# Factor rows written by transposes, and scores and weighings of stick-breaking attention taken in groups

## The reference, cut to what matters

```python
def rmsnorm_2(x, gain):
    y = xf * lax.rsqrt(jnp.mean(xf * xf, axis=-1, keepdims=True) + EPS)
    return (y * gain.astype(jnp.float32)).astype(x.dtype)

def stick_breaking_attention(q, k, v):      # (B, H, S, dh)
    for t0 in range(0, seq, Q_BLOCK):       # Q_BLOCK = 128
        t1 = t0 + Q_BLOCK
        z = jnp.einsum('bhqd,bhkd->bhqk', q[:, :, t0:t1], k[:, :, :t1]) * scale
        causal = jnp.arange(t1)[None, :] < (t0 + jnp.arange(Q_BLOCK))[:, None]
        log_stay = jnp.where(causal, jax.nn.log_sigmoid(-z), 0.0)
        log_between = lax.cumsum(log_stay, axis=3, reverse=True) - log_stay
        weights = jnp.where(causal, jnp.exp(jax.nn.log_sigmoid(z) + log_between), 0.0)
        outs.append(jnp.einsum('bhqk,bhkd->bhqd', weights, v[:, :, :t1]))

def stick_breaking_mixer(h, w_qkv, q_gain, k_gain, w_o):
    q, k, v = jnp.split(h @ w_qkv, 3, axis=-1)
    q = rmsnorm_2(q.reshape(bsz, seq, SB_HEADS, SB_HEAD_DIM), q_gain)
    k = rmsnorm_2(k.reshape(bsz, seq, SB_HEADS, SB_HEAD_DIM), k_gain)
    ...
    return o @ w_o
```

## Time and profile before

| | |
|---|---|
| median of three runs | 1926.21 us |
| the profiled execution's own time | 1931.22 us |
| its span, first to last instruction | 1929.4 us |
| TensorE busy in the span | 1885.6 us (98%) |
| VectorE busy | 1062.4 us (55%) |
| ScalarE busy | 840.9 us (44%) |
| GpSimd busy | 1084.4 us (56%) |
| mean granted TensorE clock | 0.996 of full speed |

### The profile page before, as it was taken

The page is one execution under the profiler, slowest core; times in us unless marked ns, Lnnn a source line. Parts: engine busy times, 40 slices in busy tenths (PEclk is TensorE's granted clock), DMA queues, the critical chain, the costliest instruction groups (busy, mean ns, idle before and its releaser), DMA issues.

```text
span 1929.4 us, 28543 instructions
## 1 busy us (share of the span) xinstructions
PE 1885.6 (98%) x10584; PEld 1586.1 (82%) x10584; DVE 1062.4 (55%) x1911; ACT 840.9 (44%) x1514; POOL 1084.4 (56%) x1321
## 2 busy tenths in 40 slices
PE   7998999999999999999999999999999999999998
PEld 6887777888888877777888889878887888899887
DVE  6548675632123366676756565385745576555552
ACT  4554444532233356565543444343333354444441
POOL 5327333445557433334788888654333268888882
PEclk9999999999999999999999999999999999999999
DMA  6214212223333311112233333333222133232331
GB/s 184 62 33 121 55 46 58 63 71 98 99 104 109 88 56 55 55 45 70 84 103 106 100 99 100 102 95 88 60 61 66 45 98 99 88 110 88 97 112 55
DMA packets 269163, 160.43 MB, mean 83 GB/s; under 512 B 6137, under 2 KB 267489, under 8 KB 268898
## 3 DMA queue, kind: packets, MB, share of 16 engines
q1 hardware_dynamic: 269026, 158.61, 28.5%
HBM read 156.50 MB, written 2.10 MB: 82 GB/s over the span
## 4 chain that ended last, share of the span: by engine, by line
PE 87%; POOL 5%; DVE 4%; ACT 3%; issue 2%; DMA 0%; SPq 0%; ACTq 0%; DVEq 0%
PE bank L259 20%; PE bank L1999 9%; PE bank L623 7%; PE bank L625 7%; PE bank L624 7%; POOL weight_lo L241 3%; PE bank L1600 3%; PE bank L2644 3%; PE bank L2646 3%; PE bank L2645 3%; PE bank L425 2%; PE bank L1602 2%; PE bank L1601 2%; PE bank L427 2%; PE bank L426 2%
## 5 line engine op out<-in xcount | busy, mean ns | idle before, releaser
L241 POOL TENSOR_TENSOR weight_lo<-weight_stage,weight_hi 128x256 fp32r<-128x256 f32 x1160 | 960.9, 862 | 764.0 <-ACT weight_hi L229 764.0
L229 ACT ACTIVATE weight_hi<-weight_stage 128x1024 fp32r<-128x1024 f32 (+2 forms) x303 | 309.1, 1022 | 254.7 <-PE bank L259 181.8
L259 PE MATMUL bank<-hidden_hi,weight_lo 128*128 128x512 f32 x512 | 200.4, 391 | 4.9 <-POOL weight_lo L241 4.9
L623 PE MATMUL bank<-a_hi,weight_lo 128*128 128x512 f32 (+1 forms) x464 | 198.8, 428 | 1.6 <-DVE a_lo_rounded L1137 1.0
L259 PE MATMUL bank<-hidden_lo,weight_hi 128*128 128x512 f32 x512 | 199.4, 389 | 0.0
L259 PE MATMUL bank<-hidden_hi,weight_hi 128*128 128x512 f32 x512 | 199.2, 389 | 0.0
L625 PE MATMUL bank<-a_hi,weight_hi 128*128 128x512 f32 (+1 forms) x464 | 182.8, 394 | 0.0
L624 PE MATMUL bank<-a_lo_rounded,weight_hi 128*128 128x512 f32 (+1 forms) x464 | 182.6, 394 | 0.0
L1975 POOL TENSOR_TENSOR block_weight_lo<-block_weight,block_weight_hi 128x256 fp32r<-128x256 f32 x156 | 124.7, 832 | 52.6 <-ACT block_weight_hi L2134 52.6
L2349 DVE TENSOR_TENSOR x_t<-x_t,bank 128x512 f32<-128x512 f32 x128 | 82.1, 678 | 90.4 <-PE bank L259 90.4
L259 PEld LDWEIGHTS bank<-hidden_hi,weight_lo 128*128 128x128 f32 x512 | 96.1, 188 | 26.1 <-issue 6.9
(11 more groups left out here) (393 smaller groups left out, 4407.3 us busy)
## 6 DMA issues: line engine op xcount, KB each, us to landing
weight_stage<-in_mlp_w SPq DMA_DIRECT2D x128, 512.0 KB, 3.8
weight_stage<-in_w_in SPq DMA_DIRECT2D x57, 512.0 KB, 3.7
weight_stage<-in_hg_w_in SPq DMA_DIRECT2D x32, 512.0 KB, 3.9
weight_stage<-in_sb_w_qkv SPq DMA_DIRECT2D x24, 512.0 KB, 3.6
weight_stage<-in_w_mkv SPq DMA_DIRECT2D x8, 512.0 KB, 3.8
weight_stage<-in_w_out SPq DMA_DIRECT2D x8, 512.0 KB, 3.9
weight_stage<-in_sb_w_o SPq DMA_DIRECT2D x8, 512.0 KB, 3.7
weight_stage<-in_hg_w_o SPq DMA_DIRECT2D x8, 512.0 KB, 3.7
```

Source lines behind the costliest of these rows:

```text
L229: act.activation(self.hi[slot][:, 0:size], self.stage[slot][:, 0:size], ACT.Copy).then_inc(self.hi_done, 1)
L241: last = pool.tensor_tensor(self.lo[slot][:, part], self.stage[slot][:, part], self.hi[slot][:, part].bitcast(F32), ALU.subtract)
L259: last = pe.matmul(out, l, r, start=n == 0, stop=n == 3 * len(pairs) - 1)
L623: pe.matmul(to, wlo, ahi(k), start=k == 0, stop=False)
```

## The change

In all four places that write factor rows `pe.matmul(to, column, eye, ...)` becomes `pe.transpose(to, column, eye)`; operands and results are the same. In stick-breaking, `score` of block 0 also does the scores of block 1 of the same pair, which go beside it in the bank (from column 128), and there is no score in step i = 0. TensorE's `weigh` runs in steps with i = 1 and i = 3 alone, for steps m-3 and m-2, right behind the score. VectorE masks four items in step i = 3 and none in step i = 0; `lower` moves from step i = 1 to i = 3, `put` on ScalarE from i = 0 to i = 2. Waits count accordingly.

```diff
@@ FoldedNorm.pe_spread
         for i in range(NT):
-            last = pe.matmul(self.bank[:, i * P:(i + 1) * P], self.rstd[:, i:i + 1].to_broadcast([P, P]), self.S.eye,
-                             start=True, stop=True)
+            last = pe.transpose(self.bank[:, i * P:(i + 1) * P], self.rstd[:, i:i + 1].to_broadcast([P, P]), self.S.eye)
@@ Columns.spread, spread_k and spread_out: the same edit
...
@@ stick_breaking, TensorE
+        def score_at(i):
+            return P if i == 1 else 0
...
                 wait(pe, sig, 4 * m)
-                for a in range(0, (i + 1) * P, 2 * P):
...
+                for i in (0, 1) if i == 0 else (i,):
+                    for a in range(0, (i + 1) * P, 2 * P):
...
+                            last = pe.matmul(score_banks[r][:, score_at(i) + a:score_at(i) + b],
+                                             qt[p % 3][rows, i * P:(i + 1) * P],
+                                             kt[p % 3][rows, a:b], start=True, stop=True)
...
-                if m + 1 < M:
+                if m + 1 < M and i:
                     score(m + 1)
+                if i % 2 and m >= 3:
+                    weigh(m - 3)
+                    weigh(m - 2)
                 fill(3 if some == 3 else 3 - some)
...
-                if m >= 1:
-                    weigh(m - 1)
...
+            weigh(M - 2)
             weigh(M - 1)
@@ VectorE
-                dve.wait_ge(scored, n + 1)
+                dve.wait_ge(scored, n + 3 if i == 0 else n + 1)
...
-                if i == 1 and p >= 1:
+                if i == 3 and p >= 1:
                     lower(p - 1)
                 weigh(2 * m)
-                if m + 1 < M:
-                    mask(2 * m + 2)
-                    mask(2 * m + 3)
+                if m + 1 < M and i:
+                    for n in range(2 * m + 2, 2 * m + (6 if i == 3 else 4)):
+                        mask(n)
                 weigh(2 * m + 1)
@@ ScalarE
-                act.wait_ge(masked, n + 1)
+                act.wait_ge(masked, n + 3 if i == 0 else n + 1)
...
-                if i == 0 and p >= 1:
+                if i == 2 and p >= 1:
                     put(p - 1)
```

More of the change, by code:

```diff
@@ L481, in spread @@
         for i in range(count):
-            last = pe.matmul(bank[0:rows, i * P:(i + 1) * P], self.rstd[:, first + i:first + i + 1].to_broadcast([P, rows]),
-                             self.S.eye, start=True, stop=True)
+            last = pe.transpose(bank[0:rows, i * P:(i + 1) * P],
+                                self.rstd[:, first + i:first + i + 1].to_broadcast([P, rows]), self.S.eye)
         return last
@@ L1629, in spread_k @@
                 for i in range(NT):
-                    last = pe.matmul(aux[:, i * P:(i + 1) * P], wide[:, i * P:(i + 1) * P], S.eye, start=True,
-                                     stop=True)
+                    last = pe.transpose(aux[:, i * P:(i + 1) * P], wide[:, i * P:(i + 1) * P], S.eye)
                 last.then_inc(spread, 1)
@@ L1645, in score @@
                 wait(pe, sig, 4 * m)
-                for a in range(0, (i + 1) * P, 2 * P):
[L1647 to L1653, removed]
+                for i in (0, 1) if i == 0 else (i,):
+                    for a in range(0, (i + 1) * P, 2 * P):
+                        b = min(a + 2 * P, (i + 1) * P)
+                        for r in range(2):
+                            rows = slice(r * 64, r * 64 + 64)
+                            last = pe.matmul(score_banks[r][:, score_at(i) + a:score_at(i) + b],
+                                             qt[p % 3][rows, i * P:(i + 1) * P],
+                                             kt[p % 3][rows, a:b], start=True, stop=True)
+                            if b == (i + 1) * P:
+                                last.then_inc(scored, 1)
             def turn(n):
@@ L1782, in vector @@
             scale_k(0)
-            mask(0)
-            mask(1)
+            for n in range(4):
+                mask(n)
             for m in range(M):
@@ L1856, in sigmoids @@
                 p, a = h // 2, T - (i + 1) * P
-                src = score_banks[n % 2][:, 0:(i + 1) * P]
-                act.wait_ge(masked, n + 1)
+                src = score_banks[n % 2][:, score_at(i):score_at(i) + (i + 1) * P]
+                act.wait_ge(masked, n + 3 if i == 0 else n + 1)
                 wait(act, turned, n - 3)
@@ L2715, in spread_out @@
                 for c in range(NT):
-                    last = pe.matmul(aux[:, c * P:(c + 1) * P], rstd[:, h % 2 * NT + c:h % 2 * NT + c + 1].to_broadcast([P, P]), S.eye,
-                                     start=True, stop=True)
+                    last = pe.transpose(aux[:, c * P:(c + 1) * P],
+                                        rstd[:, h % 2 * NT + c:h % 2 * NT + c + 1].to_broadcast([P, P]), S.eye)
                 last.then_inc(spread, 1)
```

2 lines of the change are left out of this document (1 added, 1 removed).

## The result

| | before | after |
|---|---|---|
| median, six runs each | 1929.17 us | 1913.39 us |
| lowest and highest | 1925.66 and 1932.79 | 1906.42 and 1917.26 |
| ratio, with its 95% interval | | 0.9914 [0.9888, 0.994] |
| the profiled execution | 1931.22 us | 1908.62 us |
| idle TensorE in stick-breaking | 2.04 us | 4.75 us |

The changed kernel is faster by 0.9%, where 1.3% was forecast: 1913.4 us against 1902.0, and 2.4 us beyond the upper end of the range. The two profiled executions are 22.6 us apart, near the 24.2 of the sum. Two executions, one of e1_rows_only (7012 us at a granted clock of 0.255) and one of the kernel before beside it (9250 us at 0.191), are left out of all figures.

What follows compares the result with a forecast made beforehand. TensorE, busy in 98% of the span, was taken to bound the kernel. 13.4 + 11.8 - 1.0 = 24.2 us off 1931.2 gives 1907.0, less 5.0 for the runs' median: 1902.0 us, range 1897 to 1911.

Steps and rivals of the forecast that it cites:

- the 24.2 of the sum: Whole kernel: factor rows 13.4 us plus groups 11.8 us, less 1.0 us for waits, gives 24.2 us saved.
- Four calls: Factor rows: a spread of four calls costs 0.88 us as matmuls and should cost 0.44 us as transposes.
- a score of blocks 0 and 1: Stick-breaking: the grouped score costs about 1.04 us with one fixed part, saving 0.40 us in each of 8 pairs.
- one direct neighbour: Stick-breaking: a product right behind a score saves one form change, 0.19 us in 14 places, 2.7 us; bounds nothing to 5.3.
- that rival: Stick-breaking: VectorE's moved work stalls every pair at `turn` in step i = 0, losing 12 us, ending at 1913 us; chance 0.08.
- the prediction's own signs of being wrong: TensorE waiting for VectorE in early pairs, a group with more than one fixed part, or a stage clock under 1.00.
- what it was plus 0.9 us: Outside stick-breaking: TensorE's idle time stays as before, but for 0.9 us more at 146 to 163 us.
- the sum was 15.3 us before waits: Stick-breaking: the forecast's terms there, 3.5 us from spreads and 11.8 us from groups.
- 1.0 charged: Stick-breaking: TensorE's waits go from 2.0 to 3.0 us; bounds a gain of 2.0 us and a loss of 4 us.
- What is late next is VectorE: Stick-breaking: VectorE's weights for `turn` come up to 1.5 us later, covered up to pair 5, not fully in pairs 6 and 7.
- a chance as a disaster: Rival: each of 33 transpose groups sets off a clock fall of 1.7 us, costing 55 us, ending at 1957 us; chance 0.02.
- The median of the runs is 5.0 us lower: Base: 5.0 us taken off the profiled execution's forecast of 1907.0 us, to predict a median of 1902.0 us.

Runs made afterwards that it cites:

- e1_rows_only: Kernel before with only the factor rows written by transposes instead of float32 matmuls; 1919.5 us, ratio 0.9939.
- e7: Changed kernel with one projection step put between the score and the products with v behind it; 1914.19 us, ratio 0.9917 to the kernel before.
- e5: Changed kernel with GpSimd waiting, ahead of splitting weight unit 25, until VectorE has made its first two biases; 1907.29 us.
- e9: Kernel before with only GpSimd's wait for VectorE's first two biases added; 1925.31 us, ratio 0.9966.
- e12: Changed kernel with scores one step at a time as before, products with v still grouped, factor rows by transposes; 1912.32 us.
- e8: Changed kernel with scores still grouped, but products with v one step at a time as before; 1914.03 us.
- e4: Changed kernel measured once more, without edits, beside other variants; 1908.45 us, ratio 0.9891 to the kernel before.
- e2: Changed kernel with the factor rows written by float32 matmuls again, so the groups alone; 1925.44 us, ratio 0.996 to the kernel before.
- e3: Changed kernel with groups up to pair 5 and the old order in pairs 6 and 7; 1913.43 us, ratio 0.9897 to the kernel before.
- e6: Changed kernel with, in the last pair, transposes of v ahead of the score and `put` and `lower` a step earlier; 1908.89 us.

## Why the prediction was right and where it was wrong

**Right: the mechanism, and nearly every price.** TensorE's list of work set the end. Four calls cost 0.44 us; a score of blocks 0 and 1 costs 1.05 us with one fixed part (1.71 with its six transposes in e7, less 0.66; forecast about 1.04); products for blocks 2 and 3 alone 1.87 (1.84); one direct neighbour saves 0.18 to 0.20 (0.19). No early pair waits for VectorE, so that rival is out. One of the prediction's own signs of being wrong did come: the clock of the stage is 0.99. Idle time outside the stage did not stay what it was plus 0.9 us either: it fell from 41.8 to 38.4 us, and 3.2 us of that is TensorE's wait for the held addition, which of the two profiles only before's has. So the question is what the 24.2 us left out.

**Terms that were left out or too small.** In the stage the sum was 15.3 us before waits; 10.39 came.

- Waits: 1.0 charged. Idle time went from 2.04 to 4.75 us, which is 2.7. "What is late next is VectorE" named one of four waits, 1.44 us at `turn`, rightly. It said that the waits of the scores would be gone, and one for ScalarE is there, 1.08 us long. And it missed the largest. I had followed `lower` to `out_bank` ("but `out_bank` is written again only in step i = 3"), and not to who reads its result. From pair 6 on the filler is the output projection, and that reads `sb_o_lo`. The timeline after of TensorE and VectorE shows it:

```profile
858.56 0.68 DVE L1784 TENSOR_TENSOR sb_o_lo<-bank,sb_o_hi 128x512 fp32r<-128x512 f32 x1
...
859.30 0.50 PE L424 MATMUL bank<-sb_o_hi,weight_lo 128*128 128x512 f32 x1 [1.74 <-DVE sb_o_lo L1784]
```

- A neighbour lost: in six steps `sums` stood right ahead of a product with v, and now stands alone. Before, the two together cost 2.90 us; apart 1.79 and 1.22, 0.11 more. That is 0.6 us, not costed.
- The clock: a stretch of 3.4 us at half clock, 1.7 us lost. The prediction gave it a chance as a disaster and no term as a small loss, though the earlier trace rows showed what one costs.

15.3 - 2.7 - 0.6 - 1.7 = 10.3 us, which accounts for the 10.39 measured. Behind the stage, 0.8 of the spreads' 4.8 us went into a wait of the scan that is new, in two places, and the clock was at half for 6.8 us at 1250 where before had 3.4 at 1273, 1.7 us more. That leaves 2.3 us, as measured. The wait after, and the stretch in a window:

```profile
PE bank L2649 <- DVE hg_q L2483: 0.8, 2, 0.4
```

```profile
1250.60:1257.40 6.80, 6.80 (x21) 5.66 (x21) 3.38 (x13) 1.06 (x1) 2.79 (x4) 0.51 0.26 76
```

Ahead of the stage it is the clock again: at 30 to 45 us after's profile has it at 0.77, before's at 0.89 (windows):

```profile
30.00:45.00 15.00, 14.38 (x70) 11.64 (x71) 8.43 (x26) 2.91 (x5) 6.59 (x10) 0.89 0.41 106
```

```profile
30.00:45.00 15.00, 14.04 (x59) 10.81 (x60) 7.33 (x24) 3.20 (x6) 5.12 (x7) 0.77 0.43 106
```

That is 0.12 x 15 = 1.8 us. 5.0 - 1.8 + 6.8 for the held instruction is 10.0 us, against 9.90 measured.

Such stretches differ from run to run, so over all runs the means tell more. Together: 24.2 - 1.7 (waits beyond the 1.0) - 0.6 - 0.8 = 21.1 us at equal clock, and some 3 us less for the clock (the mean granted one is 0.9945 over after's twelve runs, 0.9959 over before's 32; 0.0014 x 1907 = 2.7; without any held instruction, e5 and e9, it is 0.9958 and 0.9972, the same difference). That gives 18.4 us, and the kernels with the pause are 18.0 apart. That they agree to 0.4 us is luck in part: the runs with the pause tell their difference to a microsecond or two.

**The step that failed most: the base.** "The median of the runs is 5.0 us lower" treated a difference of one profiled execution and three runs as a constant. It was two kinds of execution. Before's profiled one was held, and two of its three runs, by their times, were not. So 1926.21 us was the time of an execution that is not held, and the sum from it could only give another such: with the terms as measured 1926.2 - 18.4 = 1907.8 us, which does lie in the lower bunch. The six runs of the comparison have a median of 1929.17 us, 3.0 higher than the 1926.21 that the sum rested on; after's six fell two into the lower bunch and four into the upper. The miss of 11.4 us is thus 5.8 us of terms (24.2 against 18.4), 3.0 us of base, and 2.6 us, the rest, that I put down to how many of after's runs were held. The chain of before, of which the forecast used one row at 142.63 us, goes through the held instruction 30 us later (start, length, engine, what it writes, line):

```profile
173.94 5.50 DVE first_columns L1063
```

Who had asked why a column of 128 numbers takes 5.50 us on the path would have widened the range.

## What stays open

Whether the 3.4 us at half clock in the stage follow from a wait is not shown. Of the 14 profiles, 7 of the 8 with the scores of pair 6 grouped have such a stretch between 825 and 848 us, and none of the 6 others. It does not go with the sum of the waits: e12 has as much idle time in the stage as the changed kernel (4.8 us) and no stretch, and e8 has 2.0 us and a stretch. One wait does go with it. All 8 have TensorE idle for 0.5 us ahead of `sums` of pair 6, where none of the 6 others is, and in the 7 the stretch begins 1.5 to 3.3 us behind it (in after's profile the wait ends at 825.8 us and the stretch begins at 827.4). e7, the one exception, has this wait too and keeps full clock. No run took the wait away and left the scores grouped. What makes the stretches ahead of the stage and in the scan come and go from run to run is open as well. Nor is it shown why VectorE's addition is held in one run and not in another: it starts within 0.1 us of a GpSimd instruction in both profiles above.

## To carry to other kernels

Count fixed prices of a form of the array by starts, and count them for every pair of neighbours that an edit makes or breaks, not only for those it means to make. When a step is moved, follow each of its outputs to every reader, the filler's too. Before a sum is set against a median, look for an instruction on the path that is far longer than its size allows: times that fall into two bunches have a cause in the trace, and it is the first thing to price.

## What the runs showed of the hardware

- VectorE's addition of a 128x1 column, both inputs in SBUF, takes 0.16 us with GpSimd pausing, 0.70 to 0.78 us beside its splits (after, e4, e12), and 5.5 us when it is held until eight more of them have ended. In all seven profiles in which it was held (before, e1, e2, e3, e6, e7, e8) it took 5.5 to 5.6 us. The Trainium skill (SBUF — State Buffer, section Who interferes with whom) says that a VectorE instruction with two SBUF inputs contends with a GpSimd one that reads SBUF, and that the two share a port pair that is an exclusive lock. The 0.78 us agree: a split takes 0.73 us. In the 5.5 us VectorE lost to eight instructions in succession.
- A change of the array's form costs 0.18 to 0.20 us at full clock, also from 64 rows by 128 columns straight to 128 by 64 (e7).
- A float32 call as a transpose takes half the time of the same call as a matmul (0.11 against 0.22 us by starts), and 130 calls of them did not lower the clock: its mean is 0.9958 over e1's runs and 0.9959 over before's. In e1's profile the stretches at half clock, but for one at the very end of either, are 17.0 us long in all, in before's 13.6, one of 3.4 us more.
